# Sample attention: each page of keys or values into one half of the partitions, two neighbouring keys to a partition

## The reference, cut to what matters

```python
lp = logf_past.astype(F32)
rel = lax.cumsum(lp, axis=1, reverse=True) - lp          # sum of the log forget gates behind a key
s_past = jnp.einsum('bqhd,bkhd->bhqk', q, k_past) * scale
s_past = s_past + cn[..., None] + rel.transpose(0, 2, 1)[:, :, None, :]
p = jax.nn.softmax(jnp.concatenate([s_past, s_new], axis=-1), axis=-1)
o = jnp.einsum('bhqk,bkhd->bqhd', p[..., :P], v_past)
```

## Time and profile before

| | |
|---|---|
| median of 3 runs | 4249.42 us (4246.87 to 4255.56) |
| the profiled execution | 4257.8 us, of it 4256.2 us span |
| TensorE busy | 3672.3 us, 86% |
| DVE, ACT busy | 1705.5 us, 1393.0 us |
| moved by DMA | 627.33 MB, of it the values' queue 136.48 MB |
| mean granted TensorE clock | 0.928 |

### The profile page before, as it was taken

The page is one execution under the profiler, slowest core; times in us unless marked ns, Lnnn a source line. Parts: engine busy times, 40 slices in busy tenths (PEclk is TensorE's granted clock), DMA queues, the critical chain, the costliest instruction groups (busy, mean ns, idle before and its releaser), DMA issues. The chain is left out here.

```text
span 4256.2 us, 59725 instructions
## 1 busy us (share of the span) xinstructions
PE 3672.3 (86%) x17940; PEld 2612.2 (61%) x17940; DVE 1705.5 (40%) x3173; ACT 1393.0 (33%) x2381; POOL 371.2 (9%) x630
## 2 busy tenths in 40 slices
PE   7999799879999948999999577599996968959998
PEld 6888588645555534444444155488874746748887
DVE  3222311145545433333333167433334654653333
ACT  3111200033443313332333045433335655642222
POOL 0000000010000010333333211000000000000000
PEclk9999899979999959999999788699997989979999
DMA  4323522212102067999999545533324324242221
GB/s 146 125 104 133 158 94 98 79 31 41 20 20 40 6 158 249 365 367 343 356 374 345 175 156 194 179 123 123 123 102 154 124 91 144 80 153 84 84 87 69
DMA packets 376368, 627.33 MB, mean 147 GB/s; under 512 B 125369, under 2 KB 175201, under 8 KB 376162
## 3 DMA queue, kind: packets, MB, share of 16 engines
q1 hardware_dynamic: 334386, 488.63, 34.6%
q0 software_dynamic: 41792, 136.48, 9.2%
HBM read 489.75 MB, written 135.22 MB: 147 GB/s over the span
## 5 line engine op out<-in xcount | busy, mean ns | idle before, releaser
L123 PE MATMUL in_ps_z<-in_w_hi,in_u_hi 128*128 128x512 f32 x952 | 374.7, 394 | 35.6 <-DVE in_w_lo L156 35.6
L124 PE MATMUL in_ps_z<-in_w_lo,in_u_hi 128*128 128x512 f32 x952 | 373.9, 393 | 0.0
L125 PE MATMUL in_ps_z<-in_w_hi,in_u_lo 128*128 128x512 f32 x952 | 373.6, 392 | 0.0
L1528 PEld LDWEIGHTS samp_ps_t<-samp_ident,samp_k_ring 128*128 128x128 f32 x2048 | 229.3, 145 | 179.6 <-issue 110.8
L1528 PE MATMUL samp_ps_t<-samp_ident,samp_k_ring 128*128 128x128 f32 x2048 | 282.6, 286 | 53.2 <-DMA samp_k_ring<-cache_k 50.3
L1287 POOL DMA_DIRECT2D samp_v_ring<-cache_v x512 | 274.9, 537 | 543.2 <-issue 540.4
L1561 PE MATMUL samp_ps_o<-samp_v_ring,samp_prob_t 128*64 128x512 f32 x1024 | 262.2, 636 | 25.4 <-DMA samp_v_ring<-cache_v 22.3
L1394 DVE COPY samp_kt<-samp_ps_t 128x512 f32<-128x512 f32 x256 | 173.6, 688 | 271.7 <-PE samp_ps_t L1528 268.8
L841 PE MATMUL fox_ps_o<-fox_prob,fox_v_one 128*65 128x512 f32 (+3 forms) x640 | 276.5, 529 | 0.0
L710 ACT ACTIVATE fox_prob<-fox_ps_k 128x512 f32<-128x512 f32 (+1 forms) x320 | 170.4, 533 | 256.6 <-DVE fox_ps_k L762 143.6
L1320 ACT COPY samp_kt<-samp_ps_t 128x512 f32<-128x512 f32 x256 | 145.1, 584 | 269.1 <-PE samp_ps_t L1528 269.0
(11 more groups left out here) (365 smaller groups left out, 6727.0 us busy)
## 6 DMA issues: line engine op xcount, KB each, us to landing
samp_k_ring<-cache_k SPq DMA_DIRECT2D x512, 256.0 KB, 5.8
samp_v_ring<-cache_v POOLq DMA_DIRECT2D x512, 256.0 KB, 5.2
tail_a_hi<-a_hi SPq DMA_DIRECT2D x34, 512.0 KB, 5.8
tail_a_lo<-a_lo SPq DMA_DIRECT2D x34, 512.0 KB, 6.2
in_w_stage<-w_in_even SPq DMA_DIRECT2D x64, 256.0 KB, 6.6
lru_u_hi<-u_hi SPq DMA_DIRECT2D x8, 2048.0 KB, 7.9
lru_u_lo<-u_lo SPq DMA_DIRECT2D x8, 2048.0 KB, 13.6
in_x<-x SPq DMA_DIRECT2D x17, 512.0 KB, 4.0
```

Of the source, the lines that this page charges most:

```text
L123: pe.matmul(out, act_hi, w_hi, start=start, stop=False)
L124: pe.matmul(out, act_hi, w_lo, start=False, stop=False)
L125: return pe.matmul(out, act_lo, w_hi, start=False, stop=stop)
L1528: last = pe.transpose(ps_t[:, p, a * PAGE:(a + 1) * PAGE], k_ring[:, r, p, a * P:(a + 1) * P], ident[:, :])
```

## The change

A page no longer goes to 128 partitions with one key in each. It goes to 64 partitions (`half` of them, 0 to 63 for even pages of a group, 64 to 127 for odd ones), and a partition gets two neighbouring keys, 2i and 2i+1, which lie side by side in DRAM, in one piece of 4 KB. The two keys go to the slots of two neighbouring pages in the ring, so a pair of pages fills a pair of slots, and slot u of the pair holds the keys 2i+u of both pages. What follows:

- A transpose needs both pages of the pair: there is one semaphore `k_in` for two pages, and SyncE waits for both slots at the first page of a pair.
- The gates must stand in the keys' new order. They are stored as [batch, part, head, u, page, i], so the subtraction on DVE splits even and odd keys apart (it reads with a stride), the stores double in number with pieces of half the size (256 B), and the loads double as well: four per chunk, 16 partitions, two pieces of 512 B each.
- The values' buffer is laid out so that a pair of pages fills neighbouring slots; issue order and waits of the values are as before.

The instructions of TensorE, ACT and DVE in `sample_attn` are the same in number and shape.

```diff
@@ -952,8 +952,10 @@
                 sp.wait_ge(low, r + 1)
                 for n in range(2):
                     for b in range(P // NP):
-                        sp.dma_start(io["rel"][r * (P // NP) + b, n].rearrange("h g k -> g h k"),
-                                     cut[b * NP:(b + 1) * NP, r % 2, n].bitcast(F32)).then_inc(rel_stored[r % 2], 16)
+                        for u in range(2):
+                            half = slice(u * (PAGE // 2), (u + 1) * (PAGE // 2))
+                            sp.dma_start(io["rel"][r * (P // NP) + b, n, :, u].rearrange("h g i -> g h i"),
+                                         cut[b * NP:(b + 1) * NP, r % 2, n, :, half].bitcast(F32)).then_inc(rel_stored[r % 2], 16)
             for h in range(H):
                 sp.wait_ge(added, h + 1)
                 sp.dma_start(io["new_ret_sample"][:, h].rearrange("b d e -> d b e"), new[:, h % 2]).then_inc(new_stored[h % 2], 16)
@@ -964,7 +966,7 @@
             for x in range(2):
                 sp.wait_ge(new_stored[x], 16 * H // 2)
             for x in range(2):
-                sp.wait_ge(rel_stored[x], 16 * (R // 2) * 2 * (P // NP))
+                sp.wait_ge(rel_stored[x], 16 * (R // 2) * 4 * (P // NP))
 
         @block.gpsimd
         def _(pool):
@@ -1023,7 +1025,7 @@
             def cut_high(r):
                 act.wait_ge(behind, r + 1)
                 if r >= 2:
-                    act.wait_ge(rel_stored[r % 2], 16 * 2 * (P // NP) * (r // 2))
+                    act.wait_ge(rel_stored[r % 2], 16 * 4 * (P // NP) * (r // 2))
                 act.copy(cut[:, r % 2, 0], rel[:, r % 2]).then_inc(high, 1)
 
             cut_high(0)
@@ -1049,7 +1051,9 @@
                                        lf[:, x].rearrange("p h k -> p (h k)"), 0.0, ALU.mult, ALU.add).then_inc(summed, 1)
                 dve.wait_ge(summed, r + 1)
                 dve.wait_ge(totalled, r + 1)
-                dve.tensor_tensor(rel[:, x], ps_r[:, :].unsqueeze(2).broadcast_to([P, H, PAGE]), incl[:, x], ALU.subtract).then_inc(behind, 1)
+                halves = [P, H, 2, PAGE // 2]
+                dve.tensor_tensor(rel[:, x].rearrange("p h (u i) -> p h u i", u=2), ps_r[:, :].unsqueeze(2).unsqueeze(3).broadcast_to(halves),
+                                  incl[:, x].rearrange("p h (i u) -> p h u i", u=2), ALU.subtract).then_inc(behind, 1)
                 dve.wait_ge(high, r + 1)
                 dve.tensor_tensor(cut[:, x, 1], rel[:, x], cut[:, x, 0].bitcast(F32), ALU.subtract).then_inc(low, 1)
 
@@ -1121,7 +1125,7 @@
         cum_new = ph.sb("cum_new", [H, ROWS])
         bias_new = ph.sb("bias_new", [P, NB, NS])
         k_ring = ph.sb("k_ring", [P, RING, KG, W])
-        v_ring = ph.sb("v_ring", [P, 2, KG, 2, W])
+        v_ring = ph.sb("v_ring", [P, 2, 2, KG, W])
         v_new = ph.sb("v_new", [NS, 2, W])
         rel = ph.sb("rel", [4 * H, 2, G], F32R)
         kt = ph.sb("kt", [P, 2, PAIRS, G])
@@ -1157,7 +1161,7 @@
         bd_zeroed = ph.sem("bd_zeroed")
         setup = ph.sem("setup")
         set_pe = ph.sem("setup_pe")
-        k_in = [[ph.sem(f"k_in{x}_{p}") for p in range(KG)] for x in range(RING)]
+        k_in = [[ph.sem(f"k_in{x}_{m}") for m in range(KG // 2)] for x in range(RING)]
         rel_in = [ph.sem(f"rel_in{x}") for x in range(2)]
         v_in = [[ph.sem(f"v_in{x}_{y}") for y in range(2)] for x in range(2)]
         v_new_in = [ph.sem(f"v_new_in{x}") for x in range(2)]
@@ -1190,6 +1194,10 @@
         out_kept = ph.count("out_kept")
         pe_passed = ph.sem("pe_passed")
 
+        def two_keys(cache, page):
+
+            return cache[bass.ds(page, 1)].rearrange("o (i u) n -> (o i) u n", u=2)
+
         def chunks(eng, body):
 
 
@@ -1244,18 +1252,22 @@
 
                 def group(j, x):
                     for p in range(KG):
-                        sp.wait_ge(*turned.at(t, (j - RING) * KG + p))
+                        half, both = p % 2, slice(p // 2 * 2, p // 2 * 2 + 2)
+                        if half == 0:
+                            sp.wait_ge(*turned.at(t, (j - RING) * KG + p + 1))
                         page = sp.value_load(pages[0:1, bass.ds(t * NP + j * KG + p, 1)], min_val=0, max_val=io["n_pool"] - 1)
-                        sp.dma_start(k_ring[:, x, p, :], row(io["cache_k"], page)).then_inc(k_in[x][p], 16)
+                        sp.dma_start(k_ring[half * HD:(half + 1) * HD, x, both, :], two_keys(io["cache_k"], page)).then_inc(k_in[x][p // 2], 16)
 
                 def chunk(c, q, x):
                     group(2 * c, 2 * x)
                     group(2 * c + 1, 2 * x + 1)
                     sp.wait_ge(*scored.at(t, 2 * (c - 2) + 1))
                     for y in range(2):
-                        sp.dma_start(rel[y * 2 * H:(y + 1) * 2 * H, x, :].bitcast(F32),
-                                     io["rel"][bass.ds(t, 1), :, :, bass.ds((2 * c + y) * KG, KG), :].rearrange("o n h g k -> (o n h) (g k)"))\
-                            .then_inc(rel_in[x], 16)
+                        for m in range(2):
+                            sp.dma_start(rel[y * 2 * H:(y + 1) * 2 * H, x, m * 2 * PAGE:(m + 1) * 2 * PAGE]
+                                         .rearrange("r (u k) -> r u k", u=2).bitcast(F32),
+                                         io["rel"][bass.ds(t, 1), :, :, :, bass.ds((2 * c + y) * KG + 2 * m, 2), :]
+                                         .rearrange("o n h u w i -> (o n h) u (w i)")).then_inc(rel_in[x], 16)
 
                 chunks(sp, chunk)
 
@@ -1284,7 +1296,9 @@
                         for p in range(2 * y, 2 * y + 2):
                             for g in range(2):
                                 page = pool.value_load(pages[0:1, bass.ds(t * NP + c * VC + g * KG + p, 1)], min_val=0, max_val=io["n_pool"] - 1)
-                                pool.dma_start(v_ring[:, x, p, g, :], row(io["cache_v"], page)).then_inc(v_in[x][y], 16)
+                                half = p % 2
+                                pool.dma_start(v_ring[half * HD:(half + 1) * HD, x, g, 2 * y:2 * y + 2, :], two_keys(io["cache_v"], page))\
+                                    .then_inc(v_in[x][y], 16)
 
                 chunks(pool, chunk)
 
@@ -1521,7 +1535,7 @@
 
             def turn_page(t, j, q, r, p):
 
-                pe.wait_ge(k_in[r][p], 16 * (t * (NKG // RING) + q + 1))
+                pe.wait_ge(k_in[r][p // 2], 32 * (t * (NKG // RING) + q + 1))
                 done = k_odd if p % 2 else k_even
                 pe.wait_ge(*done.at(t, (j - 1) * (KG // 2) + p // 2))
                 for a in range(PAIRS):
@@ -1531,7 +1545,7 @@
             def score(t, par, c, q, x, y):
                 j = 2 * c + y
                 if y == 0:
-                    pe.wait_ge(rel_in[x], 32 * (t * (NVC // 2) + q + 1))
+                    pe.wait_ge(rel_in[x], 64 * (t * (NVC // 2) + q + 1))
                     pe.wait_ge(*s_kept.at(t, c - 1))
                     pe.matmul(ps_s[:, :], sel_r[:, :], rel[:, x, :], start=True, stop=False, skip_group_check=True)
                 pe.wait_ge(*k_even.at(t, j * (KG // 2) + 1))
@@ -1559,7 +1573,7 @@
                 for p in range(2 * y, 2 * y + 2):
                     for g in range(2):
                         last = pe.matmul(ps_o[g * HT:(g + 1) * HT, :],
-                                         prob_t[:, x, g, p, :], v_ring[:, x, p, g, :], start=is_chunk(c, 0) and p == 0,
+                                         prob_t[:, x, g, p, :], v_ring[:, x, g, p, :], start=is_chunk(c, 0) and p == 0,
                                          stop=is_chunk(c, NVC - 1) and p == KG - 1 and g == 1, skip_group_check=True)
                 last.then_inc(weighed.sem, 1)
 
@@ -2816,7 +2830,7 @@
 
 
 SCRATCH = dict(fq=[T, P, W], rq=[T, P, W], rk=[T, P, W], rv=[T, P, W], g0=[T, P, G], g1=[T, P, G], u_hi=[T, P, D], u_lo=[T, P, D],
-               neg_cum=[2, H, PT, P], fo=[T, P, W], ro=[P, W], rel=[NB, 2, H, 64, PAGE], a_hi=[T, P, D], a_lo=[T, P, D], h=[T, P, D])
+               neg_cum=[2, H, PT, P], fo=[T, P, W], ro=[P, W], rel=[NB, 2, H, 2, 64, PAGE // 2], a_hi=[T, P, D], a_lo=[T, P, D], h=[T, P, D])
 RESULTS = dict(y=[T, P, D], fk=[T, P, W], fv=[T, P, W], new_logf=[T, P, H], new_ret_prompt=[H, HD, HD], new_ret_sample=[NB, H, HD, HD],
                lru_h_prompt=[P, KC], lru_conv_prompt=[P, KC, 3], lru_h_sample=[P, KC, NB], lru_conv_sample=[P, KC, NB, 3])
```

## The result

The change makes the kernel slower: 4624.84 us (median of 4 runs) against 4251.74 us, a ratio of 1.087 with a 95% interval of 1.086 to 1.089, or +373 us. The forecast was 4500 us with a range of 4340 to 4630, so the result lies 5 us inside the upper end.

A forecast was written before the change was run, and what follows sets the result against it. The DMA engines (11.6 us per chunk) were taken to bound sample attention, just ahead of TensorE (10.5). The terms 235 + 18 + 3 + 2 - 6 = +252 us on 4249 gave about 4500 us, range 4340 to 4630.

The forecast's parts named there:

- the signs: Expected profile of sample attention: DMA share near 1 at 250 to 290 GB/s, chunks about 16 us, TensorE's clock below 1.
- What bounds the kernel: Sample attention: DMA engines at 11.6 us per chunk, just ahead of TensorE at 10.5; SyncE's queue in the first batch.
- Edit 1: Pages into 64 partitions, steady part: half the bytes at 212 GB/s, half at 363; +235 us, bounds 0 and +470.
- Edit 2: Keys in 4 KB instead of 2 KB packets, sample attention: 0.1 us per chunk, 6 us saved in all.
- Edit 3: SyncE's longer key loads and doubled gate loads: 13.1 us per chunk, nothing in the steady part, +18 us in first batch.
- Edit 4: GpSimd's value loads over 64 partitions: no change per page; +3 us for bunching in the last batch, range 0 to +17.
- Edit 5: Sample attention: waits for both pages of a pair hidden by loads in flight; 512 B gate pieces cost nothing.
- Edit 6: Stage writing the past gates: strided subtraction costs nothing, doubled stores hidden by a gap; +2 us, range 0 to +8.
- (a): Sample attention: halves don't hurt, SyncE's queue bounds at 13.1 us per chunk; +96 us, 4345 us; chance 0.09.
- (b): Sample attention: engines stay in step, both streams crowd one half; +470 + 23, about 4740 us; chance 0.06.
- (c): Sample attention faster: piece count or memory side bounds DMA, halves alternate freely; about 4215 us; chance 0.08.
- (d): Sample attention unchanged: pieces and halves both hidden, a chunk stays at 11.7 us; 4250 us; chance 0.07.

The follow-up runs named there:

- e5: The kernel before, with the two gate loads of a chunk issued from ScalarE's queue instead of SyncE's: 4236.14 us, ratio 0.996.
- e7: The kernel before, with a chunk's gates in four loads of 1 KB rows on SyncE's queue instead of two, same bytes: 4312.49 us, ratio 1.014.
- e6: The changed kernel, with its four gate loads of a chunk issued from ScalarE's queue instead of SyncE's: 4528.91 us, ratio 1.064.
- e1: The kernel before, with a load-only stage ahead: ten sections varying partitions, piece size and queues (3: alternating halves, one queue); 203 to 381 GB/s, no kernel time given.
- e9: The kernel before, with keys in 4 KB pieces into partitions 32 to 95 (half unread), values whole, four gate loads on ScalarE's queue: 4262.73 us, ratio 1.003.
- e3: The changed kernel, with values whole and every key page into partitions 32 to 95 (half unread), gate loads still on SyncE: 4441.69 us, ratio 1.045.

## Why the prediction was right in sign and range, and where it was short

The sign was right, and for the reason given: half of the partitions, half of the rate. The size was put at +252 us and is +373. That the range holds is in part luck. The forecast's own 4400 to 4610 was missed, and the upper end of 4630 was kept for stretches of TensorE at 1.2 GHz that would make it late. Its clock averaged 0.83 to 0.85 and it was not late; SyncE's queue, put at nothing in the steady part, filled that room. Of the signs, the rate (228 to 252 GB/s) fell below the 250 to 290 named, and a chunk takes 17.8 us, not 16.

**What bounds the kernel: half right.** DMA "in front" of TensorE held (e5: 366 GB/s once nothing else hinders). But I took SyncE's round, 10.1 us, from the end of the first batch for all batches. Earlier in that batch there are rounds of 11.8 us (1597.73 to 1609.52), and in the later batches a round takes about as long as the chunk itself; e7 shows that it bound the kernel together with the DMA engines. The sign to look for was there: a queue that issues for 620 us and waits for 8.3.

**Edit 1, the halves: right mechanism, one rate too high.** +235 us were put, from 212 GB/s on one half and 363 on opposite ones. The first was 203, the second 298. 2.13 / 203 + 2.13 / 298 gives 17.6 us per chunk instead of 15.9; 17.8 was measured. That these two are so close is partly chance, since the 17.8 has SyncE's queue in it: with the gates off SyncE a chunk takes 17.1 (e6). The assumption that failed is that alternate halves soften the cost as much as put, because pages in flight let the engines drift apart (e1, section 3: 225 GB/s). The choice between the bounds was right, "today's rate" for the opposite halves was not. Between e9 and e6, which differ in the halves (keys from 32 to 95 into halves, values from whole into halves), lie 266 us; between e3 and the change, which differ in the same way with the gates on SyncE, lie 183. The 235 us lie between these two.

**Edit 2, 4 KB pieces: nothing to see.** Put at -6 us. Two queues of whole pages make 368 GB/s, two of 4 KB pieces in partitions 32 to 95 make 368 as well (e1, sections 6 and 10).

**Edit 3, SyncE's queue: the largest miss.** The key load over 64 partitions took 469 ns, not 587 (in e1, where addresses are fixed as in the earlier trace rows, such loads into 0 to 63 and the alternating halves take a median of 597), but each of the four gate loads some 600 where I had 0.45 with what lies between:

```profile
L1259 SPq DMA_DIRECT2D samp_k_ring<-cache_k x512: 468/469/1187, 1582.6 to 2665.9; - x171
...
DMA to landing us min/median/max: 3.2/15.3/29.5
```

(the tile `k_ring` of the changed kernel, ns min/median/max). In the first batch the two errors cancel in some rounds, 13.0 us from 1676.55 to 1689.51 us where 13.1 was forecast, but others take up to 15.5:

```profile
1604.84 2.55 SPq L1267 DMA_DIRECT2D samp_rel<-rel  x4
1608.42 10.01 SPq L1259 DMA_DIRECT2D samp_k_ring<-cache_k  x8
1620.30 2.88 SPq L1267 DMA_DIRECT2D samp_rel<-rel  x4
...
1676.55 2.55 SPq L1267 DMA_DIRECT2D samp_rel<-rel  x4
1679.86 9.60 SPq L1259 DMA_DIRECT2D samp_k_ring<-cache_k  x8
1689.51 2.53 SPq L1267 DMA_DIRECT2D samp_rel<-rel  x4
```

The mean of the seven rounds from 1591.79 us on is 14.0 us, 10.9 before. From the first load of keys to the first multiplication with values it takes 124.7 us, 98.3 before: +26 where +18 was put. Up to 1640 us the halves are in it as well (DMA share 1.04 to 1.06 at 221 to 231 GB/s).

In the steady part, where I let it "cost nothing" because 13.1 is below 15.9, it works 14.6 us of 17.8, and cost 96 us (change against e6); with the halves out of the way it costs 179 (e3 against e9). This is the term that the prediction put at nothing. The reason that fits the waits: the gate loads stand ahead of the next keys in the queue and wait for the gates' buffer (164.8 us), and behind that wait there is too little time to fill the ring again. In e6 the ring is kept full, and only slots are waited for. That this is the mechanism is argued from the two wait rows; the 96 us are measured. Some 11 of them belong to the first batch (124.7 us against 113.4 in e6).

**Edit 4 and the last batch: about right.** GpSimd's busy time per load went from 536 to 512 ns. From the last gate load to the last load of values it took 90.4 us before and 91.6 after (+3 was put).

**Edit 5: small.** It is at most the 27 us by which e9 is slower than e5, and these have the longer key loads and edit 6 inside. Its own share was not measured.

**Edit 6, the stage before: right.** The strided subtraction takes 1225 ns, 1224 before. The stores fill SyncE's queue until 1555.0 us, the next is at 1557.95, and the first load of keys starts at 1582.6 instead of 1579.6, of which 1.6 us had come up before this stage (+2 was put).

**The rivals.** (a) was no rival but the second half of the answer: +192 us if alone (e3). (b), all in step on one half, did not occur: two queues on opposite halves reach 298. The whole kernel took 4625 us, not 4740. (c) and (d) are out. TensorE's clock fell to 0.83 to 0.85, the level at which its work was forecast to stay hidden; with DMA waits of 224 us its work is not what is late.

The ledger, from medians: kernel before 4249; all else of the change 14 (e9); the halves 266 (e6 less e9); the gate loads on SyncE 96 (change less e6). Together 376; measured 373.

These shares hang on the order in which the two costs are taken away. With the halves gone first they are 183 us (change less e3), and the gate loads on SyncE are 179 (e3 less e9), again 376 with the 14. Either cost without the other leaves the kernel slower than before by more than its smaller share: 276 us with the halves (e6), 192 with the queue (e3), the 14 in both. The two overlap, and neither split is the true one. What is shown is that together they make all but 14 us, and that both must go to win the time back.

## What to carry to other kernels

Two transfers into opposite halves of the partitions are no substitute for one transfer over all: keep each transfer on all of them, or on a 64 that straddles the middle (32 to 95 ran at 355 GB/s, 0 to 63 at 203). Ask of each issuing queue how long it waits, not only how busy the DMA engines are: a queue that never waits may be a bound, even where the DMA share reads 100%. Take its round from the rounds that matter, not from a few of the first batch. And where two costs overlap, take them away in both orders before you give either a price.

## What the runs showed of the hardware that I had not expected

- Alternating the halves on one queue hardly helps: 24 such loads made 225 GB/s, against 203 on one half, with all engines busy (1.02 and 1.03).
- Which 64 partitions are written changes the time that the load holds SyncE's queue, with page numbers read from the table: 469 ns median for halves, 512 for 32 to 95 (e3), 333 for all 128. Gate loads of 16 partitions and 32 pieces took some 600 ns, against 332 for 16 pieces, of 2 KB before and of 1 KB in e7 alike.
- A queue of whole pages with 2 KB rows made 320 GB/s by itself with 0.91 of the engines busy, one of page pairs with 4 KB rows 381. The loads differ in size too (256 and 512 KB), and the first was the first section to run, so the row's length is not shown to be the cause. With two queues whole pages and 4 KB pieces both made 368.
